# Sums of an output projection begun inside the last attention step, and weight splitting moved from GpSimd to VectorE

## The reference, cut to what matters

```python
h = rms_norm(x, g_pre_a)                      # 544 rows of 1024
q, k, v, gate = split(h @ w_in_a, 4)          # 1024 x 4096
q, k = rms_norm(q, g_q), rms_norm(k, g_k)     # per head
z = q k^T / 8;  log_stay = where(mask, log_sigmoid(-z), 0)
w = where(mask, exp(log_sigmoid(z) + sum of log_stay over later keys), 0)
o = w v
x = x + (silu(gate) * o) @ w_o_a              # 1024 x 1024: the output projection
```

## Time and profile before

| What | us |
|---|---|
| Median of the runs (lowest, highest) | 838.37 (836.5, 839.04) |
| The profiled execution | 835.96 |
| Its span, first to last instruction | 833.7 |
| PE busy in the span | 778.6 (93%) |
| DVE busy | 452.3 (54%) |
| ACT busy | 348.5 (42%) |
| POOL busy | 311.7 (37%) |
| POOL, subtraction of weights, 80 pieces | 190.7 |

### The profile page before, as it was taken

How to read it: one execution, slowest core, us unless ns; L and a number is a source line. 1 busy time by engine, 2 the same in 40 slices (tenths; PEclk the granted TensorE clock), 3 DMA queues, 4 the chain that set the end, 5 groups by cost and what they waited for, 6 DMA issues and landing times.

```text
span 833.7 us, 13594 instructions
## 1 busy us (share of the span) xinstructions
PE 778.6 (93%) x4623; PEld 662.9 (80%) x4623; DVE 452.3 (54%) x1025; ACT 348.5 (42%) x886; POOL 311.7 (37%) x262
## 2 busy tenths in 40 slices
PE   5689999999999999978999889999999999999996
PEld 4688898979898889846878877999777787876785
DVE  6556666675767585873145432214766655656222
ACT  6444434443444443451168343323445343446211
POOL 5344353434444343560213445442534243443100
PEclk9899999999999999979999999999999999999999
DMA  7630303030303030313023242231201002030211
GB/s 220 155 103 26 110 27 109 26 111 25 109 25 109 25 109 25 103 47 136 26 83 94 93 148 92 67 117 32 70 23 45 24 26 77 26 96 6 108 50 57
DMA packets 68082, 61.68 MB, mean 74 GB/s; under 512 B 7144, under 2 KB 55040, under 8 KB 68032
## 3 DMA queue, kind: packets, MB, share of 16 engines
q1 hardware_dynamic: 68032, 61.04, 23.8%
HBM read 50.85 MB, written 10.17 MB: 73 GB/s over the span
## 4 chain that ended last, share of the span: by engine, by line
PE 59%; issue 14%; DVE 11%; POOL 9%; ACT 3%; DMA 2%; SPq 2%; POOLq 0%; DVEq 0%; ACTq 0%
PE bank L417 13%; PE bank L419 12%; PE bank L418 12%; POOL wlo L1487 4%; DVE stay L1766 4%; POOL rstd L1550 3%; PE bank L1012 2%; PE bank L1014 2%; PE bank L1013 2%; PE bank L996 2%; PE bank L968 2%; PE bank L966 2%; PE bank L710 1%; PE bank L688 1%; PE bank L946 1%
## 5 line engine op out<-in xcount | busy, mean ns | idle before, releaser
L1487 POOL TENSOR_TENSOR wlo<-raw,whi 128x1024 fp32r<-128x1024 f32 (+3 forms) x80 | 190.7, 2391 | 119.5 <-ACT whi L1099 119.4
L417 PE MATMUL bank<-whi,hthi 128*128 128x384 f32 (+1 forms) x360 | 130.2, 362 | 3.2 <-DVE wlo L1701 2.6
L419 PE MATMUL bank<-whi,htlo 128*128 128x384 f32 (+1 forms) x360 | 126.2, 351 | 0.0
L418 PE MATMUL bank<-wlo,hthi 128*128 128x384 f32 (+1 forms) x360 | 126.1, 350 | 0.0
L1099 ACT ACTIVATE whi<-raw 128x1024 fp32r<-128x1024 f32 (+3 forms) x84 | 82.6, 1007 | 33.5 <-PE bank L419 29.7
L1766 DVE TENSOR_TENSOR_SCAN stay<-stay 128x512 f32<-128x512 f32 (+4 forms) x72 | 78.2, 1086 | 11.8 <-ACT stay L1194 11.8
L1550 POOL TENSOR_TENSOR rstd<-msq,neg_half 128x4 f32<-128x4 f32 x40 | 40.3, 1008 | 105.8 <-DVE msq L1733 104.9
L417 PEld LDWEIGHTS bank<-whi,hthi 128*128 128x128 f32 x360 | 69.6, 193 | 9.1 <-issue 7.4
L417 PE MATMUL bank<-hthi,whi 128*128 128x272 f32 x256 | 75.0, 293 | 0.0
L419 PE MATMUL bank<-hthi,wlo 128*128 128x272 f32 x256 | 73.6, 287 | 0.0
L418 PE MATMUL bank<-htlo,whi 128*128 128x272 f32 x256 | 73.5, 287 | 0.0
(11 more groups left out here) (198 smaller groups left out, 1690.3 us busy)
## 6 DMA issues: line engine op xcount, KB each, us to landing
raw<-in_w_in_a SPq DMA_DIRECT2D x64, 256.0 KB, 3.1
raw<-in_w_in_b SPq DMA_DIRECT2D x24, 256.0 KB, 3.7
raw<-in_w_o_a SPq DMA_DIRECT2D x16, 256.0 KB, 2.8
raw<-in_w_kv_b SPq DMA_DIRECT2D x16, 256.0 KB, 3.1
raw<-in_w_o_b SPq DMA_DIRECT2D x16, 256.0 KB, 3.0
raw<-in_w_q_b SPq DMA_DIRECT2D x16, 192.0 KB, 2.4
x_in<-in_x_prompt SPq DMA_DIRECT2D x4, 512.0 KB, 5.0
out<-qkn SPq DMA_DIRECT2D x8, 256.0 KB, 2.4
```

Of the source, the lines that this page charges most:

```text
L417: eng.matmul(dst, st[0], mv[0], start=(k == 0), stop=False)
L418: eng.matmul(dst, st[0], mv[1], start=False, stop=False)
L419: mm = eng.matmul(dst, st[1], mv[0], start=False, stop=(k == n - 1))
L1487: nc.gpsimd.tensor_tensor(wlo[slot][:, c], raw[:, c], whi[slot][:, c].bitcast(F32), ALU.subtract).then_inc(s_lo, 1)
```

## The change

The low parts of groups 1 to 9, made at the entries W, move from POOL to DVE, in the same place of the list. Step 7 walks a list of its own (`LAST_A`), with nine entries E: they hold parts k = 0 to 6 of the sums 0, 1 and 2, in blocks of two, two and three parts (6, 6 and 9 matmuls), each with a wait for the high and low part of that pair. After step 7 PE makes parts 0 to 6 of sum 3, then part 7 of sums 0 to 3, then the other six sums. The sums use banks 0, 1, 7, 2, 3, 0, 1, 2, 3, 0. In the first half the sample's tile comes last; DVE adds in that order. Two lists of banks of the next stage are permuted.

```diff
+EARLY = 3
+FIRST = [1, 2, 3, 4, 0]
+LAST_A = [("S", 0), ("S", 1), ("W", 0), ("E", 0), ("T", 0), ("S", 2), ("E", 1), ("W", 1), ("W", 2), ("T", 1),
+          ("O", 0), ("S", 3), ("E", 2), ("T", 2), ("S", 4), ("W", 3), ("E", 3), ("O", 1), ("T", 3), ("S", 5),
+          ("E", 4), ("T", 4), ("S", 6), ("E", 5), ("O", 2), ("T", 5), ("S", 7), ("E", 6), ("T", 6), ("S", 8),
+          ("E", 7), ("T", 7), ("E", 8), ("T", 8), ("O", 3), ("O", 4)]
+
+def early(e):
+    r, third = e // 3, e % 3
+    return [(r, k) for k in ((0, 1), (2, 3), (4, 5, 6))[third]]
+
+def order_a(ahead):
+    return STEP_A if ahead else LAST_A
...
-        LAB, QAB = [bank[2], bank[0], bank[1]], [bank[1], bank[0]]
+        RES = [bank[b] for b in (0, 1, 7, 2, 3, 0, 1, 2, 3, 0)]
+        RES_FREE = [0, 0, 0, 0, 0, 1, 2, 4, 5, 6]
+        LAB, QAB = [bank[2], bank[1], bank[0]], [bank[0], bank[1]]
...
# TensorE
+            def residual(n, ks):
+                nh, tile = n // TT, ORDER[FIRST[n] if n < TT else n - TT]
+                for k in ks:
+                    if k == 0:
+                        weights(G_OA + nh)
+                        if n < EARLY:
+                            pe.wait_ge(s_zeros_b, 2)
+                            pe.wait_ge(s_dve_c, CA * NP)
+                            pe.wait_ge(s_xev, XA * NP)
+                        if RES_FREE[n]:
+                            pe.wait_ge(s_x2sum, RES_FREE[n])
+                    if n <= EARLY:
+                        pe.wait_ge(s_ghi, k + 1)
+                        pe.wait_ge(s_glo, k + 1)
+                    st = [acol(gt[0], k, tile), acol(gt[1], k, tile)]
+                    mv = [wcol(G_OA + nh, m, k, 0, 512, 512) for m in range(2)]
+                    pe.matmul(RES[n][:, :], st[0], mv[0], start=(k == 0), stop=False)
+                    pe.matmul(RES[n][:, :], st[0], mv[1], start=False, stop=False)
+                    mm = pe.matmul(RES[n][:, :], st[1], mv[0], start=False, stop=(k == KD - 1))
+                if ks[-1] == KD - 1:
+                    mm.then_inc(s_yprod, 1)
...
+                        elif what == "E":
+                            for r, k in early(n):
+                                residual(r, [k])
...
-            weights(G_OA)
-            weights(G_OA + 1)
-            pe.wait_ge(s_ghi, NP - 1)
-            pe.wait_ge(s_glo, NP - 1)
-            pe.wait_ge(s_zeros_b, 2)
             pe.wait_ge(s_stay, UA * NP)
+            residual(EARLY, range(KD - 1))
+            for n in range(EARLY + 1):
+                residual(n, [KD - 1])
+            for n in range(EARLY + 1, TT):
+                residual(n, range(KD))
             for i in range(TT):
-                residual(i, 0)
-            for i in range(TT):
-                residual(i, 1)
+                residual(TT + i, range(KD))
                 if i:
                     turn_x2(i - 1)
...
# GpSimd, step_a
-                    elif what == "W":
-                        if n == 0 and not (isinstance(p, int) and p < 0):
-                            sem, count = last_reader(p + 2)
-                            pool.wait_ge(sem, count)
-                        split_piece(p + 2, n, par, KD * 512)
...
# VectorE
+            def weight_lo(g, j, slot):
+                c = slice(j * KD * 512 // PIECES, (j + 1) * KD * 512 // PIECES)
+                dve.wait_ge(s_hi, PIECES * g + j + 1)
+                v.tensor_tensor(wlo[slot][:, c], raw[:, c], whi[slot][:, c].bitcast(F32),
+                                ALU.subtract).then_inc(s_lo, 1)
+
             def step_a(p, par, att=True, ahead=True):
-                for what, n in STEP_A:
-                    if what == "C" and ahead:
+                for what, n in order_a(ahead):
+                    if what == "W":
+                        if n == 0 and not (isinstance(p, int) and p < 0):
+                            sem, count = last_reader(p + 2)
+                            dve.wait_ge(sem, count)
+                        weight_lo(p + 2, n, par)
+                    elif what == "C" and ahead:
...
-                m = TT * nh + i
+                m = TT + i if nh else FIRST.index(i)
...
-                v.tensor_tensor(x2[0:n, t, c], bank[m % 4][0:n, :], x2[0:n, t, c], ALU.add).then_inc(s_x2sum, 1)
+                v.tensor_tensor(x2[0:n, t, c], RES[m][0:n, :], x2[0:n, t, c], ALU.add).then_inc(s_x2sum, 1)
...
-            for i in range(TT):
+            for i in FIRST:
                 add_x(i, 0)
```

More of the change, by code:

```diff
@@ L768, in _ @@
             step_a(7, 1, ahead=False)
[L770 to L785, removed]
             def turn_x2(i):
@@ L1784, in gate_out @@
                                 ALU.mult).then_inc(s_odone, 1)
-            def step_a(p, par, att=True, ahead=True):
-                for what, n in STEP_A:
-                    if what == "C" and ahead:
+            def weight_lo(g, j, slot):
[3 more added lines that the diff above has]
+                                ALU.subtract).then_inc(s_lo, 1)
+            def step_a(p, par, att=True, ahead=True):
+                for what, n in order_a(ahead):
+                    if what == "W":
[4 more added lines that the diff above has]
+                    elif what == "C" and ahead:
                         if not att and n + 3 < TT:
```

## The result

The changed kernel takes 812.75 us (median of four runs, 810.2 to 814.22), the kernel before 837.43 (four runs, 835.22 to 839.04). The ratio is 0.9704, with an interval of 0.9669 to 0.9739: 24.7 us faster. The sign and the mechanism came out as forecast, and the gain came where it was forecast, but for 2.4 us behind the sums, where none was.

What follows compares the result with a forecast made beforehand. PE was taken as the bound, losing time to waits for DVE, which POOL stretches, and to a low clock. Gains of 11.0 + 5.5 + 2.3 = 18.8 us gave 819.5 us, range 813 to 826.

Steps and rivals of the forecast that it cites:

- the steps' waits: Attention steps, 60 to 358 us: PE's 14 waits for `wgt`, together 5.5 us, all go.
- what follows sum 4: Behind sum 4 (split of next weights, norms, turns): everything keeps its distance from it, no gain.
- the way from the profiled execution to the median: Whole kernel: median of timed runs lies 2.4 us above the profiled execution, so 817.2 becomes 819.6.
- The low parts on DVE: Groups 1 to 9: 36 pieces of about 1.22 us on DVE, each giving back about 2.0 us.
- The first stage: Last input tile's normalisation no longer stretched beside POOL's piece: 2.3 us gained, between 2.1 and 4.0.
- The last step and its sums: Three sums begin early: 14.6 us of matmuls move in, step 3.6 us longer at 28.1, net gain 11.0.
- The idleness before the first transpose: Last attention step: PE still idle 0.6 us there after one block of six matmuls.
- Blocks on the attention's chain: Rival, last step: early blocks hold up the attention, 6 of the 11 us go, 825.5 us; chance 0.14.
- A low clock there: Rival, last step: PE at clock 0.50 for some 20 us, half of that lost, 829 us; chance 0.06.
- The 5.5 us that don't come: Rival, attention steps: another engine's result is late at the same place, no step gain, 825 us; chance 0.07.
- DVE as the bound: Rival, attention steps: pieces before units 3 and 4 delay PE from about 3.1 us each, 845 us; chance 0.03.
- More comes: Rival: clock does not fall at the start and nothing idles in the last step, 815 us; chance 0.12.

Runs made afterwards that it cites:

- the other two: Two repeat runs of the unaltered changed kernel, each with a profile: 810.64 us (0.9693) and 813.35 us (0.9722).
- the second profile: The kernel before, run once more unaltered with a profile: 835.35 us (0.9992 of itself).

## Why the prediction was right in kind and 6.75 us short

The mechanism held, part by part. What failed are three terms of the sum: the steps' waits, taken at 5.5 us (7.05 came); what follows sum 4, put at nothing (2.4 came); and the way from the profiled execution to the median, put at 2.4 (nothing came). Each alone is more than the 0.25 us by which the range was missed.

**The low parts on DVE**: right. 1.22 us a piece, no stretched instruction, `wgt` in time. **The first stage**: right in size, by some luck; 2.3 was taken, between 2.1 and 4.0, and S0 of pair 0 came 2.4 us earlier in the first profile, 3.6 and 3.7 in the other two. Counted from the normalisation of the last input tile, which itself came at other moments, it is 1.7, 4.4 and 3.2: the granted clock from 20 to 60 us was 0.91 in the first of these profiles, as in the kernel before, and 0.96 in the other two. **The last step and its sums**: right; 28.1 forecast and 28.2 measured, and 11.0 against 10.84 to the fifth add. (The idleness before the first transpose, put at 0.6, is 1.80 less six matmuls of 0.232, which is 0.4; 0.38 was measured.) That the gain came out so near is in part luck, since it is counted from the first profile of the kernel before, where the last step up to ScalarE's high part took 24.9 us. The fall of the clock there can be longer: the second profile took 27.12 at 0.74, and against that one the gain to the fifth add is 14.5:

```profile
357.87:384.99 27.12, 18.31 (x106) 11.10 (x105) 20.96 (x24) 11.69 (x23) 13.39 (x5) 0.74 0.16 49
```

**The steps' waits**: the mechanism was right, the term too small by 1.55 us. "I take the whole 5.5 us as gone" took the sum of PE's idle time; the seven steps got 7.05 us shorter. Per step PE's idleness fell by 0.8 us but the pitch by 1.05: from the product ahead of transpose T3 to T3 it fell by 0.45 where 0.38 had stood idle, and from S5 to T4 by 0.59 where 0.43 had the earlier trace rows: together 1.04 of the 1.05. The modelled end of the matmul in front can cover the rest: each product ahead of T3 is shown to last 0.27 us, where a pair of them starts every 0.10 us. The Trainium skill (Perfetto Trace Analysis, Tensor Engine Instruction (MATMUL, LD_WEIGHTS)) says that the end shown for TensorE is computed and not observed; these two places agree with that. So such a wait is to be read from the starts of the matmuls on either side, and not from the idle time in front of one.

**What follows sum 4 "keeps its distance"**: true up to the latent stage, wrong by 0.9 us in it (within what the kernel before varies by there) and by 1.5 in the second layer, which is one fall of the clock in code that the change leaves as it is but for two lists of banks. Why it fell in the one kernel and not in the other stays open.

**From the profiled execution to the median**: the 2.4 us added for it were the sampling of three runs. Five groups of runs of the kernel before have medians from 835.3 to 837.4, and the changed kernel's profiled run lies on its own median.

Together 1.55 + 2.4 + 2.4 = 6.35 of the 6.75 us; 0.4 is the time around the span, which was 2.2 us in the first profile and 1.8 in the new one.

**The rivals.** Blocks on the attention's chain: PE idles 0.8 us in the last step, so no. A low clock there: 1.00, so no. The 5.5 us that don't come: they came and more. DVE as the bound: its mechanism is real but its threshold was wrong. "It decides from about 3.1 us per piece" gave DVE 7.5 us of slack in a step (four times 1.9); the runs show 1.8 to 2.4, that is about 1.7 to 1.8 us a piece. At 1.22 the change stays under it, by less than the forecast thought. "More comes", 815, was nearest, though for another reason than it gave: the last step was as forecast.

## What to carry to other kernels

When an engine works in order, its busy share says nothing of its slack: lengthen one of its instructions a little, and read where the step begins to grow. Here an engine that was busy 61% of a step of 41.24 us had about 2 us to spare. Work moved between GpSimd and VectorE is to be priced by what it does to VectorE's whole busy time, stretches included, and not by the waits it ends. And a stretch of idleness is worth filling only up to its length: the third early sum brought 1.3 us, the first two together 5.9 (fifth add 49.03 us behind S0 of pair 7 without early sums, 43.14 with two, 41.87 with three).

## What the runs showed of the hardware that was not expected

POOL's work costs DVE even where nothing depends on it: 11.6 us of POOL's subtractions in a step made DVE 7.04 us busier and the step 4.64 us longer. The granted clock stays at 1.00 through a step in which PE is busy 14.25 of 21.08 us in short pieces, and falls elsewhere behind 0.91 us of idleness, or does not, with the same code in front. One and the same kernel had a fall near 575 us in one profile and none there in the other.
